# A two-block transformer layer pair on one core: the FFN's up weights taken two units at a time in seven half-size products, and the down phase reordered

## The reference, cut to what matters

```
u = causal_dwconv(rms_norm(h, ffn_norm) @ w_up, conv_w, conv_b)   # w_up: 1024 x 5632, conv width 3
gate, up = jnp.split(u, 2, axis=-1)                               # 2816 columns each
h = h + (jax.nn.silu(gate) * up) @ w_down                         # w_down: 2816 x 1024
```

## Time and profile before

| What | Value |
|---|---|
| Time of 3 runs, median (lowest, highest) | 1583.11 us (1583.02, 1587.7) |
| Profiled execution, its own time | 1583.06 us |
| Its span, first to last instruction | 1581.3 us |
| Busy share of the span: PE, PEld, DVE, ACT, POOL | 81%, 45%, 27%, 15%, 1% |
| Chain that ended last: PE, DMA | 58%, 38% of the span |
| Bytes read from HBM | 499.78 MB, 317 GB/s over the span |

### The profile page before, as it was taken

How to read it: one execution, slowest core, us unless ns; L and a number is a source line. 1 busy time by engine, 2 the same in 40 slices (tenths; PEclk the granted TensorE clock), 3 DMA queues, 4 the chain that set the end, 5 groups by cost and what they waited for, 6 DMA issues and landing times.

```text
span 1581.3 us, 17427 instructions
## 1 busy us (share of the span) xinstructions
PE 1281.0 (81%) x7251; PEld 706.3 (45%) x7251; DVE 432.2 (27%) x1021; ACT 238.9 (15%) x655; POOL 18.2 (1%) x30
## 2 busy tenths in 40 slices
PE   8999999999999999998657657667567567577577
PEld 4665788854488744544223223223223223223223
DVE  3444233383155566231101101101101101101101
ACT  3334323211022100211100100000001001001001
POOL 2000000000000000100000000000000000000000
PEclk9999999999999999999878979878879888878889
DMA  9441177413542457999999999999999999999997
GB/s 298 158 162 54 49 275 247 157 53 121 198 152 76 146 189 263 363 405 428 426 430 427 429 430 426 431 427 429 430 426 430 428 427 430 428 429 429 427 427 323
DMA packets 93416, 501.35 MB, mean 317 GB/s; under 512 B 6798, under 2 KB 34818, under 8 KB 68161
## 3 DMA queue, kind: packets, MB, share of 16 engines
q1 hardware_dynamic: 92608, 500.00, 77.9%
q0 software_dynamic: 768, 0.85, 0.4%
HBM read 499.78 MB, written 1.05 MB: 317 GB/s over the span
## 4 chain that ended last, share of the span: by engine, by line
PE 58%; DMA 38%; DVE 2%; ACT 1%; issue 1%; SPq 0%; ACTq 0%; DVEq 0%
DMA arena<-in_w 38%; PE ps L1422 17%; PE ps L1104 8%; PE ps L784 7%; PE ps L1299 6%; PE ps L779 5%; PE ps L1156 3%; PE ps L963 2%; PE ps L1351 2%; PE ps L1119 1%; PE ps L1196 1%; PE ps L805 0%; PE ps L860 0%; PE ps L1488 0%; PE ps L1232 0%
## 5 line engine op out<-in xcount | busy, mean ns | idle before, releaser
L1422 PE MATMUL ps<-arena,hT 128*32 128x512 f32 x1984 | 277.6, 722 | 254.6 <-DMA arena<-in_w 254.6
L1422 PEld LDWEIGHTS ps<-arena,hT 128*32 128x32 f32 x1984 | 69.3, 130 | 462.5 <-issue 320.8
L2350 DVE TENSOR_TENSOR moe_hid<-moe_hid,ps 64x512 f32<-64x512 f32 x32 | 22.1, 690 | 483.9 <-ACT moe_hid L2698 483.9
L1444 PE MATMUL ps<-arena,moe_turned 128*32 128x512 f32 x1024 | 116.7, 595 | 28.0 <-DVE moe_turned L2352 27.8
L1104 PE MATMUL ps<-hT,arena 128*128 128x256 f32 x640 | 138.3, 379 | 0.0
L1104 PEld LDWEIGHTS ps<-hT,arena 128*128 128x128 f32 x640 | 121.5, 190 | 16.5
L1404 PEld LDWEIGHTS ps<-sel,h 128*128 128x128 f32 x992 | 113.2, 192 | 24.1 <-issue 24.1
L2698 ACT ACTIVATE moe_hid<-ps 64x512 f32<-64x512 f32 x32 | 18.9, 590 | 656.3 <-PE ps L1422 650.4
L1404 PE MATMUL ps<-sel,h 128*128 128x64 f32 x992 | 117.2, 276 | 0.0
L784 PE MATMUL ps<-hT,arena 128*128 128x256 f32 x512 | 113.9, 380 | 0.1
L784 PEld LDWEIGHTS ps<-hT,arena 128*128 128x128 f32 x512 | 96.8, 190 | 15.0 <-issue 2.2
(11 more groups left out here) (407 smaller groups left out, 1051.9 us busy)
## 6 DMA issues: line engine op xcount, KB each, us to landing
arena<-in_w SPq DMA_DIRECT2D x184, 2048.0 KB, 29.2
arena<-in_w_in SPq DMA_DIRECT2D x18, 2048.0 KB, 8.1
arena<-in_w_up SPq DMA_DIRECT2D x22, 1024.0 KB, 7.3
arena<-in_w SPq DMA_DIRECT2D x14, 1024.0 KB, 13.1
arena<-in_w_down SPq DMA_DIRECT2D x5, 2048.0 KB, 12.2
arena<-in_w_out SPq DMA_DIRECT2D x2, 2048.0 KB, 14.3
arena<-in_w_conv_out SPq DMA_DIRECT2D x2, 2048.0 KB, 7.9
arena<-in_w_attn_out SPq DMA_DIRECT2D x2, 2048.0 KB, 7.8
```

The source lines that it names most:

```text
L1422: last = mm(ps[k * CAP:(k + 1) * CAP, UP, :], x[:, c, (k % 2) * CAP:(k % 2 + 1) * CAP], w[:, at:at + DE], start=(c == 0), stop=(c == KC - 1))
L1444: last = mm(ps[k * CAP:(k + 1) * CAP, DN, :], a[:, m * 64 + (k % 2) * CAP:m * 64 + (k % 2 + 1) * CAP], w[:, at:at + 512], start=(m == 0), ...
```

## The change

- **Up phase in sets of seven.** Unit 0 stays as it was, but its results go to PSUM banks 5 and 6. Units 1 to 10 are taken as five sets of two (`up_seven`): tokens halved in 2, the 1024 rows halved in 2, and the two units' 512 columns each as the two column halves; seven products of 4 matmuls each, 128x128 tokens against 128x512 weights. The result is there with tokens on partitions.
- **Turning back.** `turn_up(k)` brings each unit's result (`u_tok`, kept in `h`) back to channels on partitions with 8 transposes of 128x128 into freed banks; those of a set stand in the next set, behind its products 1 and 5, and those of the last set in the down phase.
- **New sums on DVE.** Once, 4 sums of tokens (`up_x_sums`, 128x512 each). Per set, 4 sums of weights of 128x2048 (t1, t3, t2, t4) and 5 sums out of PSUM of 128x512 (u2, u3, c22, c12, c21). ACT copies 2 results per set out of PSUM.
- **Convolution.** Same operations; the order of taps is changed (both halves' first tap, then both second taps), ACT reads all four parts of a unit and then does the two SiLUs, and the loops are written out.
- **Ring.** The up units go round all four slots. `up2` and `up3` wait only for the slots of `wout0` and `wout1`. The third transfer of `w_down` (1 MB) moves to behind product 6 of the last set.
- **Down phase.** The same 77 matmuls and the 16 transposes of units 9 and 10, in another order: products 1 of six pairs, a turn, products 1 of three, a turn, `products567` of two pairs, product 2 of nine, and so on; five `products567` (pairs 4 to 8) now stand one behind another.
- **Late waits and loads.** PE waits for a set's second unit at product 6. POOL's four late loads wait besides for product 1 of set 1.

The core of the diff:

```
+ORDER_UP = [1, 5, 6, 7, 2, 3, 4]
+W_SUMS_UP = ["t1", "t3", "t2", "t4"]
...
+            pool.wait_ge(seven_filled, count7(1 - UP_SETS, ORDER_UP, 1))
...
-            with nc.tensor.Fori(0, NPAIR // 2) as i:
-                for s in range(2):
-                    ffn_up(1 - s, dense_loads(u0 + s + 1) + 32 * i, 2 * i + s + 1)
+            def up_seven(m):
+                ...
+                for product in ORDER_UP:
+                    if product == 6:
+                        u = UNIT[f"up{2 * m + 2}"]
+                        pe.wait_ge(dense_loaded[RING_SLOT[u]], dense_loads(u))
+                    ...
+                    for c in range(4):
+                        ...
+                        last = mm(up_seven_bank(m, product), lhs, rhs, start=(c == 0 and product not in (2, 3)), stop=(c == 3),
+                                  skip_group_check=True)
+                        if product == 1 and c == 0:
+                            release_up(m)
+                    last.then_inc(seven_filled, 1)
+                    if m and product in (1, 5):
+                        turn_up(2 * m - 1 + (product == 5))
...
-            AHEAD = 3
...
+            for i in range(6):
+                product1(i)
+                if i == 0:
+                    release_up(UP_SETS)
+            turn_up(NPAIR - 2)
+            for i in range(6, 9):
+                product1(i)
+            turn_up(NPAIR - 1)
+            products567(0)
+            products567(1)
+            ...
+            for i in range(9):
+                product2(i)
+            products567(2)
+            products567(3)
+            for i in range(3):
+                product3(i)
+            for i in range(4, 9):
                 products567(i)
...
+            for m in range(UP_SETS):            # DVE
+                if m:
+                    up_sum(m - 1, "c21")
+                    up_w_sums(m)
+                    for a in range(2):
+                        conv_taps(2 * m - 1, a)
+                    for a in range(2):
+                        conv_gate(2 * m - 1, a)
+                conv_taps(2 * m, 0)
+                up_sum(m, "u2")
+                conv_taps(2 * m, 1)
+                conv_gate(2 * m, 0)
+                up_sum(m, "u3")
+                up_sum(m, "c22")
+                up_last_w_sum(m)
+                conv_gate(2 * m, 1)
+                if m + 1 < UP_SETS:
+                    up_first_w_sum(m + 1)
+                up_sum(m, "c12")
```

More of the change, by code:

```diff
@@ L117 @@
 RING = 4
-RING_SLOT = ([_u % RING for _u in range(U_FFN)] + [2 + _k % 2 for _k in range(FCH // 2)] + [0, 1, 3]
-             + [(2, 0, 1, 3)[_i % RING] for _i in range(len(UNITS) - U_BLK2)])
+RING_SLOT = ([_u % RING for _u in range(U_FFN)] + [(2 + _k) % RING for _k in range(FCH // 2)] + [1, 2, 3]
+             + [_i % RING for _i in range(len(UNITS) - U_BLK2)])
 NPAIR = FCH // 2
@@ L356, in two_blocks, with up_columns, up_seven_bank @@
         g_tok = cbz.rearrange("p a b -> p (a b)").rearrange("p (a n) -> p a n", a=2)
+        def up_columns(m):
+            w0, w1 = (dense_slot(f"up{k}").rearrange("p (c n) -> p c n", c=KC) for k in (2 * m + 1, 2 * m + 2))
+            return w0[:, 0:4, :], w1[:, 0:4, :], w0[:, 4:8, :], w1[:, 4:8, :]
+        def up_seven_bank(m, product):
+            return ps[:, up_bank(m) + BANK7[product], :]
         def bank7(g, product):
@@ L1092, in _ @@
             wout(1, 1, False, lambda: norm_turn(1, xn, 0))
[L1094 to L1109, removed]
             u0 = U_FFN
@@ new lines, in release_up, with turn_up @@
+            def release_up(m):
+                if m == 0:
+                    pe.wait_ge(ff_filled, 2)
+                    pe.sem_inc(dense_used, 1)
+                else:
+                    pe.wait_ge(seven_filled, count7(m - 1 - UP_SETS, ORDER_UP, 4))
+                    pe.sem_inc(dense_used, 2 if m < UP_SETS else 1)
+            def turn_up(k):
+                m, n = divmod(k - 1, 2)
+                if n == 0:
+                    pe.wait_ge(seven_sums, count7(m - UP_SETS, SUMS7, "c21"))
+                    pe.wait_ge(seven_copied, 2 * m + 2)
+                for a in range(2):
+                    for g in range(2):
+                        for half in range(2):
+                            last = turn(ps[:, conv_bank(k) + a, g * S + half * P:g * S + (half + 1) * P],
+                                        u_tok[:, half, n, (2 * g + a) * P:(2 * g + a + 1) * P], ident)
+                    last.then_inc(ff_filled, 1)
@@ L1981, in sum_weights @@
                 v.tensor_tensor(b12, b21, t2, ALU.subtract).then_inc(w_sums, 1)
-            sum_rows(0, NPAIR - 1)
+            sum_rows(0, NPAIR - 2)
+            up_sum(UP_SETS - 1, "c21")
+            dve.wait_ge(seven_sums, count7(-1, SUMS7, "c21"))
             sum_weights(0)
-            ffn_part(NPAIR - 1, 0, 0)
             sum_weights(1)
-            ffn_part(NPAIR - 1, 0, 1)
-            sum_rows(NPAIR - 1, NPAIR)
-            for i in range(2, NPAIR):
+            for k in (NPAIR - 2, NPAIR - 1):
+                for a in range(2):
+                    conv_taps(k, a)
+                for a in range(2):
+                    conv_gate(k, a)
+                if k == NPAIR - 2:
+                    sum_weights(2)
+                    sum_weights(3)
+            sum_rows(NPAIR - 2, NPAIR)
+            for i in range(4, NPAIR):
                 sum_weights(i)
@@ L2550, in _, with conv_step @@
             norm_take(1, 1)
-            def ffn_step(k, s):
+            def conv_step(k):
                 for a in range(2):
@@ L2565, in _ @@
             act.sem_inc(ff_read_act, 7)
-            with nc.scalar.Fori(0, FCH // 4) as i:
-                for s in range(2):
-                    ffn_step(2 * i + s, s)
-            ffn_step(FCH // 2 - 1, 0)
+            for m in range(UP_SETS):
+                act.wait_ge(seven_filled, count7(m - UP_SETS, ORDER_UP, 1))
+                if m:
+                    act.wait_ge(seven_sums, count7(m - 1 - UP_SETS, SUMS7, "u2"))
+                a_(r1_, up_seven_bank(m, 1), ACT.Copy).then_inc(seven_copied, 1)
+                if m:
+                    conv_step(2 * m - 1)
+                conv_step(2 * m)
+                act.wait_ge(seven_filled, count7(m - UP_SETS, ORDER_UP, 2))
+                if m:
+                    act.wait_ge(ff_filled, 4 * m)
+                a_(u_tok[:, 0, 0, :], up_seven_bank(m, 2), ACT.Copy).then_inc(seven_copied, 1)
+            conv_step(NPAIR - 2)
+            conv_step(NPAIR - 1)
             a_(tail[:, 10:11], one, ACT.Sqrt)
```

198 lines of the change are left out of this document (137 added, 61 removed).

## The result

The changed kernel took 1576.92 us, median of six runs (1574.7 to 1578.45), beside 1585.49 us for the kernel before on the same chip (1583.02 to 1587.89, six runs). The ratio is 0.9946, with a 95% interval of 0.9936 to 0.9957: 8.6 us less, between 6.8 and 10.1. The forecast was 1574.0, 9.1 less than its base.

What follows compares the result with a forecast made beforehand. PE bounds the kernel up to the experts, then a weight stream of fixed length at memory rate. 120.15 + 8.9 - 138.14 + 0 = -9.1 us, so 1583.1 becomes 1574.0 us; range 1571.8 to 1579.

Steps and rivals of the forecast that it cites:

- The sum: Whole kernel: new products and turns less the old up phase, down phase at 0, give -9.1 us, 1574.0 us.
- Products and turns: Up phase: five sets of products cost 120.15 us and ten turns 8.9, in place of 138.14.
- Rival (c): Turns: each transpose is paid at its full length, 0.273 us, giving 1587 us; chance 0.04.
- DVE's chain: Each set of the up phase: DVE finishes c22 at T + 17.9, 1.0 us ahead of product 3.
- Rival (a): Up phase: DVE's chain to c22 is 2.0 us longer, PE waits 1.0 in four sets, 1578 us; chance 0.12.
- The start: Set 0 of the up phase: `up2` lands by 185 us and t2 is ready 3.6 us ahead of product 6.
- (b): Set 0: `up2` shares the queues and lands at 194.8, product 6 waits 6.2 us, 1580.2 us; chance 0.04.
- The down phase: Down phase: DVE's sums slower than PE's `products567`, 0.9 us of new stalls at pairs 6 to 8.
- net 0: Down phase: the present 1.1 us of stalls go and new ones as large come, so no change in time.
- Rival (d): Experts' loads: bound by bytes before the stream starts, so PE's lead is given back, 1583 us; chance 0.06.

Runs made afterwards that it cites:

- e2: Changed kernel with each turn doing its eight transposes twice, into the same places; 1585.6 us, ratio 0.9997 to the kernel before.
- e4: Changed kernel with five idle additions of 0.69 us on DVE between sums u3 and c22 of every set; 1585.63 us, ratio 0.9998 to the kernel before.
- e5: Changed kernel with two idle additions of 0.69 us on DVE between sums u3 and c22 of every set; 1576.96 us, ratio 0.9949 to the kernel before.
- e1: The changed kernel again with no edit, as base for other runs; 1576.37 us, ratio 0.9948 to the kernel before.
- e9: Changed kernel with only POOL's small loads issued early again; 1575.17 us, ratio 0.9934 to the kernel before.
- e7: Changed kernel with one 2 MB load of `w_down` and its two waits for normalized tokens put ahead of `up2` and `up3`; 1582.42 us, ratio 0.9975.
- e8: Changed kernel with the first `product3` put between the five `products567` of the down phase; 1576.96 us, ratio 0.9943 to the kernel before.
- e3: Changed kernel with PE's down phase back in its old order, DVE's list unchanged; 1586.36 us, ratio 1.0004 to the kernel before.
- e6: Changed kernel with POOL's small loads early and PE waiting for both units ahead of a set, as before; 1579.65 us, ratio 0.9961.
- e11: Changed kernel with early small loads and PE waiting for both units ahead of a set, run a second time; 1576.31 us, ratio 0.9943.

## Why the prediction was right

**The sum.** Forecast -9.1 us; the stage measures -9.31 and the runs -8.6 (-6.8 to -10.1). The ratio forecast, 1574.0 / 1583.06 = 0.9943, lies in the interval. The absolute time was 2.9 low, and most of that is the base: 1583.06 was an execution without a fall of the clock ahead of the FFN, while the kernel before has medians of 1585.5 to 1586.8 over more runs. The step that was missing is how far the three runs shown stand for the kernel; their own spread, up to 1587.7, said so.

**Products and turns.** 120.15 + 8.9 were forecast. A set between turns runs at the forecast pace: sets are 25.79 apart (24.03 + two turns of 0.88). Eight turns stand in the up phase, 120.15 + 7.0 = 127.2 against 127.17 measured; the other two stand in the down phase. The gain comes from the count of products and not from their shape: the same work in eight products of 128x512 would be 160 matmuls, 137.3 us at 0.858, an estimate from these rows and only 0.8 less than the 138.14 of before, while the 20 that are left out are 17.2. Rival (c), a transpose at its full length, is refuted by e2: 0.109 us per transpose where it needed 0.225. The figure of the Trainium skill (TensorE: Matmul & The Clock Gate, Part 4: PE-mode transpose) is right for the length of one record here (0.273 us) and would have given the wrong sign as a price in a stream.

**DVE's chain.** Forecast: c22 is done 1.0 us ahead of product 3. The trace shows 1.7 and e4 1.5, and e5 stayed within it. Timeline of DVE in set 1 of the changed kernel, from T = 215.69, the end of product 4:

```profile
215.89 0.69 DVE L2100 TENSOR_TENSOR h<-moe_hid,ps 128x512 f32<-128x512 f32 x1 [2.75 <-PE ps L1183]
216.50 2.29 DVE L2073 TENSOR_TENSOR arena<-arena 128x2048 f32<-128x2048 f32 x1
218.82 2.29 DVE L2075 TENSOR_TENSOR arena<-arena 128x2048 f32<-128x2048 f32 x1
221.03 3.21 DVE L2034 SCALAR_TENSOR_TENSOR arena<-ps,arena 128x255 f32<-128x255 f32 x8
224.15 0.75 DVE L2041 TENSOR_TENSOR arena<-arena 128x256 f32<-128x256 f32 x2
226.05 1.65 DVE L2034 SCALAR_TENSOR_TENSOR arena<-ps,arena 128x255 f32<-128x255 f32 x4 [1.15 <-ACT arena L2751]
...
227.94 0.69 DVE L2100 TENSOR_TENSOR moe_turned<-moe_turned,ps 128x512 f32<-128x512 f32 x1 [0.25 <-PE ps L1183]
...
230.11 0.42 DVE L2041 TENSOR_TENSOR arena<-arena 128x256 f32<-128x256 f32 x1
231.38 0.69 DVE L2100 TENSOR_TENSOR moe_hid<-moe_turned,ps 128x512 f32<-128x512 f32 x1 [0.85 <-PE ps L1183]
232.20 0.69 DVE L2100 TENSOR_TENSOR h<-moe_hid,ps 128x512 f32<-128x512 f32 x1
```

c22 ends at 232.89 and product 3 starts at 234.61. The order is as counted, but two errors of size partly cancel. Four taps take 1.65 or less instead of the 1.90 taken from a looped half-unit, and with the rest DVE is through with the gate ahead of u3 at T + 14.8 (230.53), where the count has T + 16.45. And the count has no wait of DVE for PE: u3 stands idle for 0.85 until product 7 is through, u2 before it for 0.25. So the 1.7 us are the room of u3 and c22 alone, which PE's own product 2 (3.43 us) gives them; what stands ahead of u3 has 0.85 more, 2.6 us. That longer room is read from the trace; no run put work there. Rival (a) was further off than the 1.0 us made it look.

**The start.** Forecast: `up2` lands 3.7 us ahead of set 0 (185 against 188.65) and t2 is 3.6 ahead of product 6. Measured: t1 starts 3.73 ahead of the set, t2 ends at 194.75, 3.8 ahead of product 6 at 198.52. That the two agree so well is luck, since two terms were off and cancel. Timeline of SP's issues, kernels e1 and e9:

```profile
175.00 5.20 SPq L600 DMA_DIRECT2D arena<-in_w_up  x4
```

```profile
175.01 8.74 SPq L600 DMA_DIRECT2D arena<-in_w_up  x4
```

In e1, whose set 0 starts at 188.50 (forecast 188.65), `up2` goes out at 175.00, 2 us ahead of the 177 that the forecast used, and is there at 185.05, 10.05 us behind its issue and not 7.2. The forecast costs the moved small loads at nothing; so they do, and e9 shows that left early they would have cost 0.6 us. e7 makes (b) real for 5.9 us, by a later issue and an earlier load together.

**The down phase.** Forecast 0.9 us of new stalls at pairs 6 to 8; measured 1.05, mostly at pairs 6 and 8. Timelines of PE and of DVE, kernel after:

```profile
351.48 2.74 PE L1235 MATMUL ps<-arena 128*128 128x512 f32 x6
354.48 1.99 PE L1235 MATMUL ps<-moe_turned,arena 128*128 128x512 f32 x4 [0.26 <-DVE arena L2163]
356.30 1.02 PE L1235 MATMUL ps<-moe_hid,arena 128*128 128x512 f32 x2
...
360.16 1.98 PE L1235 MATMUL ps<-moe_turned,arena 128*128 128x512 f32 x4 [0.18 <-DVE arena L2163]
...
351.68 0.69 DVE L2160 TENSOR_TENSOR moe_turned<-arena 128x512 f32<-128x512 f32 x1 [2.25 <-PE ps L1235]
...
353.74 0.69 DVE L2163 TENSOR_TENSOR arena<-arena,moe_turned 128x512 f32<-128x512 f32 x1
```

As argued, DVE's 2.75 us (351.68 to 354.43) meet PE's 2.57. The label says 0.26, but the distance of the starts, 3.00 where 2.57 is normal, and 1.82 where it is 1.72 behind, say 0.53: read gaps as distances. Two such places are 1.06, and e8, without them, gains 1.05. Where the step fell short is its "net 0", right as a difference between the two kernels but silent on what the new order carries: without it the change is worth nothing (e3, with DVE's list as it is).

**Does it reach the end?** Yes, us for us: block 2 to the end is 1186.4 and 1186.5 us, and e2, e3 and e4 each bring back in the total (9.2, 10.0, 9.3) what they add to the stage (8.7, 9.3, 9.5). Rival (d) is refuted.

## What to carry over

When products are traded for additions, price PE by the distance of the starts of its records, and walk the helper engine's chain to its tightest reader, with the waits for PE inside it; the margin there (1.7 us behind u3, 2.6 ahead of it) and the work order behind it (up to 9.3 us, as much as the gain) decide whether the saving stands. A change of some us can be judged in the stage it touches, to 0.1 us, when totals scatter by 5; but an interval from six runs of one kernel can stand 0.2% beside that of another six runs of it, so a single slow median isn't a finding.

## What the runs showed of the hardware beyond that

A gap of PE can cost more than its length: behind e7's gap of 3.96 us the granted clock was 0.57 over the next 4 us, behind e3's of 3.68 it was 0.50 from 349 to 351, and each cost 1.8 us on top of the gap. Each was seen in one execution. Behind e4's five gaps of 1.67 us it stayed at 1.00:

```profile
238.00:244.00 6.00, 4.33 (x11) 1.00 0.00 0
```

But the length of the gap alone doesn't decide. Ahead of the FFN, between 134 and 141 us, every execution has a gap of 1.6 us. Timeline of PE, kernels e6 and e1; behind it the clock fell to 0.50 (138 to 140) in e6, which lost 1.6 us, and stayed at 1.00 in e1:

```profile
135.95 0.87 PE L937 MATMUL ps<-arena 128*64 128x256 f32 x8 [1.61 <-ACT arena L2672]
```

```profile
136.03 0.87 PE L938 MATMUL ps<-arena 128*64 128x256 f32 x8 [1.61 <-ACT arena L2675]
```

The clock also fell where PE had no gap, at 100 to 107 us (about 3 us lost), in seven of the 13 profiled executions, and in four of them also near 15 us, behind a gap of 1.3 us that the others have too. The first profile and e1 are one kernel and differ in this, and e6 and e11 are one kernel and differ at 136 us, so no edit is needed to set it off; what does stays open. These falls account for the start of the FFN: e3's two cost 1.7 and 3.2 us and make up 4.9 of the 4.95 us between its 193.45 and e1's 188.50.

Four small loads of 416 KB in all in POOL's queue (64, 64, 32 and 256 KB), issued beside the 2 MB of `up2` in SP's (e9: the first at 174.53, `up2` from 175.01), held it up by 4.0 us; SP's issues themselves take 8.74 us instead of 5.20. Why so little data costs so much was not tried.
